# A hybrid decoder step with 32 experts: the last expert's block written out behind TensorE's loop, and the samples' final sums laid over 128 partitions behind the first prompt tile's

## The chip, the cores and the metric

The kernel runs on one NeuronCore of a Trainium2 chip. Its time is the device time of one execution in microseconds (us), the median of several runs. A page of the profile and a trace come from one execution recorded by the hardware profiler. Engines: TensorE (PE, with PEld for its weight loads), VectorE (DVE), ScalarE (ACT), GpSimd (POOL) and SyncE (SP); the suffix q means the engine's sequencer (SPq issues DMAs). L12 is line 12 of the kernel.

## What is computed

One layer over 512 prompt rows and 8 sample rows (one new token for each of 8 sequences), all in float32, 1024 wide. Attention and convolution come first; they are not touched here. The part at issue is the mixture of experts and its last sum:

```python
def _layer_tail(x, attn, conv, w_out, norm2_w, router_w, router_b, ...):
    x = x + jnp.concatenate([attn, conv], axis=-1) @ w_out
    h = _rmsnorm(x, norm2_w).reshape(B * S, D)
    return x + _moe(h, router_w, router_b, w_gate_up, b_gate_up, w_down, b_down).reshape(B, S, D)

def _moe(...):          # 32 experts, each row goes to the 4 best
    gates = softmax(the 4 largest router logits of a row)
    for each expert e:  # rows that chose e
        gu = xb @ w_gate_up[e] + b_gate_up[e]         # 1024 x 2048
        act = (clip(gu[:, F:]) + 1) * min(gu[:, :F], 7) * sigmoid(1.702 * g)
        y = act @ w_down[e] + b_down[e]               # 1024 x 1024
    return sum over a row's 4 experts of gate * y
```

An expert's weights are 8 MB (gate and up) and 4 MB (down), so the 32 experts read 400 MB.

## The kernel before, in words

**Experts.** Work is organised in blocks of at most 128 rows, one block per expert (E = 32), plus up to OVF = 16 late blocks for experts that more than 128 rows chose; with these inputs there are none, but each engine still steps through a loop of 16 passes (`Fori(0, OVF)` with an `If` inside: L2122 to L2127 on DVE) and skips each body. Block i's rows are gathered from `h2_rows` in DRAM by GpSimd (`gather`, L733), multiplied by gate and up weights (`gate_up_front` L1509 for rows 0 to 63, `gate_up_back` L1528 for rows 64 to 95 and 96 to 127, skipped by `by_size` where the block has no such rows), clipped and multiplied on DVE and ACT, transposed (L1616) and multiplied by the down weights (`down_front` L1546, `down_back` L1557). DVE (`copy_y`, L2079 and L2080) and ACT (`copy_y`, L1153, eight small copies) take the result from PSUM to `y_sb`, and GpSimd scatters its rows to `y_rows` in DRAM (`scatter`, L744).

**TensorE's order.** `expert_block(i, i - 1)` does gate and up of block i, transposes the rows of block i + 1, does down of block i - 1 and transposes the activations of block i. Blocks 0 and 1 are written out, `pe.Fori(2, E)` runs blocks 2 to 31, and `down_block(E - 1, ...)` behind the loop does the last down with weights in buffers of their own (`last_down_front`, `last_dn`). DVE, ACT, POOL and SP have loops of their own over the same blocks. A down of block i waits until both `copy_y` of block i - 1 are done (`y_front`, `y_back`).

**Weights.** SP loads them in chunks of 2 MB: four chunks of gate and up (L573), two of down (L578), each waiting for its buffer (`w_used`); the last down has its own two loads (L629). Behind these SP queues five loads of the residual rows `x2_rows` into `out_acc` (L633), waits for the last down (L638), steps through the loop of 16, waits for the last scatter, and issues five loads of `y_rows` into `out_rows` (L650).

**The last sum.** `out_rows[u]` has, for each row of tile u, its 4 expert rows side by side; `gates` has the 4 gates of each row. DVE makes, for each tile u and each of the 4 choices, one `scalar_tensor_tensor`: acc = rows * gate + acc (L2135). Tiles 0 to 3 are the four prompt tiles of 128 rows, tile 4 (`TILES`) the 8 sample rows. `OUT_ORDER = [TILES] + list(range(TILES))` sets the order of the loads (SP), sums (DVE) and stores (ACT, L1175): samples first, then prompt tiles 0 to 3.

Of the kernel before, what the change touches and what calls it, by code (L numbers as in the profile page):

```python
# [7 lines left out]
P = 128  # L8
D = 1024
# [45 lines left out]
def hybrid_step(nc, x_prompt, x_sample, cache_k, cache_v, state_conv, page_table, norm1_w, w_in,  # L55
# [10 lines left out]
    with ctx:  # L66
# [140 lines left out]
        out_acc = [v_flat[:, u * D:(u + 1) * D] for u in range(TILES)] + [q_b[:, :, :].rearrange("p a n -> p (a n)")]  # L207
# [141 lines left out]
        y_stored, x2_back, gu_done = [sem(n) for n in ("y_stored", "x2_back", "gu_done")]  # L349
# [133 lines left out]
        OUT_ORDER = [TILES] + list(range(TILES))  # L483
# [5 lines left out]
        def _(sp):  # L489
# [141 lines left out]
            sp.wait_ge(late_slots_done, 1)  # L631
            for u, s in enumerate(TAIL):
                sp.dma_start(out_acc[u][0:rows_of(s), :], x2_rows[row0[s]:row0[s] + rows_of(s), :]  # L633
                             ).then_inc(x2_back, 16)
# [13 lines left out]
            for u in OUT_ORDER:  # L648
                r, m = row0[TAIL[u]], rows_of(TAIL[u])
                sp.dma_start(out_rows[u][0:m, :],  # L650
                             y_rows[r * TOPK:(r + m) * TOPK, :].rearrange("(p k) n -> p (k n)", k=TOPK)
                             ).then_inc(y_loaded[u], 16)
# [123 lines left out]
        def _(act):  # L776
# [396 lines left out]
            for no, u in enumerate(OUT_ORDER):  # L1173
                act.wait_ge(pair_done, TOPK * (no + 1))
                act.dma_start(y_out[TAIL[u]], out_acc[u][0:rows_of(TAIL[u]), :]).then_inc(y_stored, 16)  # L1175
# [3 lines left out]
        def _(pe):  # L1179
# [421 lines left out]
            def expert_block(i, before=None, front=gate_up_front, back=gate_up_back):  # L1601
# [8 lines left out]
                if before is not None:  # L1610
                    down_block(before, isinstance(i, int))
# [25 lines left out]
            with pe.Fori(2, E) as i:  # L1637
                expert_block(i, i - 1)
            down_block(E - 1, False, last_down_front, last_down_back)
# [9 lines left out]
        def _(dve):  # L1649
# [480 lines left out]
            dve.wait_ge(x2_back, 16 * (TILES + 1))  # L2130
            for no, u in enumerate(OUT_ORDER):
                m, acc = rows_of(TAIL[u]), out_acc[u]
                dve.wait_ge(y_loaded[u], 16)
                for k in range(TOPK):
                    nc.vector.scalar_tensor_tensor(acc[0:m, :], out_rows[u][0:m, k * D:(k + 1) * D],  # L2135
                                                   gates[0:m, u, k:k + 1], acc[0:m, :], ALU.mult, ALU.add
                                                   ).then_inc(pair_done, 1)
                    dve.wait_ge(pair_done, no * TOPK + k + 1)
# [44 lines left out]
```

## Time and profile before

| what | value |
|---|---|
| time, median of 3 runs | 1743.2 us (1741.07 to 1750.26) |
| profiled execution, its own time | 1743.68 us |
| its span in the trace | 1742.0 us |
| PE busy | 1464.7 us (84%) |
| DVE busy | 781.1 us (45%) |
| ACT busy | 356.1 us (20%) |
| HBM read and written | 589.36 MB and 25.87 MB |

Times inside the trace run from the span's start to 1742.0. The experts take the stretch from about 665 us to 1700 us, the last sum the 42 us behind it. Busy time is an average over stages with different limits; the waits, the chain that ended last and the DMA landings tell what a stretch is limited by.

### The profile page before, as it was taken

The numbers are of one execution on the slowest core, as the hardware profiler recorded it, in microseconds if no ns is written. First come the engines' busy times: TensorE is split into PE (matmuls) and PEld (weight loads), VectorE is DVE, ScalarE is ACT, GpSimd is POOL, SyncE is SP. The second block draws the span as 40 slices with busy tenths as digits, with TensorE's granted clock in tenths as the row PEclk, the third lists the DMA queues.
The fourth block names the chain that finished last, engine by engine and source line by source line (L and its number), as shares of the span: only waits on it lengthen the run. The fifth ranks groups of instructions, "written<-read, shape, count | busy, mean of one in ns | idle before, by whom it ended". The sixth has DMA issues, their size and how long they took to land.

```text
span 1742.0 us, 32083 instructions
## 1 busy us (share of the span) xinstructions
PE 1464.7 (84%) x11950; PEld 589.3 (34%) x11951; DVE 781.1 (45%) x1158; ACT 356.1 (20%) x822; POOL 95.4 (5%) x173
## 2 busy tenths in 40 slices
PE   3868886768898868999999898999998998998870
PEld 2433332335433343333333332332333332332220
DVE  2789877997886335211323222232232131131316
ACT  3212202232320221111211211211212122121220
POOL 0000002000000000000000000000000000000000
PEclk8989996688998857999999999999999999999995
DMA  9558798878989765579999999999999999999976
GB/s 326 190 176 270 268 356 289 262 258 282 332 295 308 253 257 216 234 312 404 428 418 415 427 399 397 426 404 395 418 423 402 410 428 394 402 428 428 427 324 251
DMA packets 127181, 598.10 MB, mean 343 GB/s; under 512 B 20392, under 2 KB 20406, under 8 KB 101915
## 3 DMA queue, kind: packets, MB, share of 16 engines
q1 hardware_dynamic: 109088, 560.20, 81.5%
q10 hardware_dynamic: 8522, 20.00, 3.2%
q0 software_dynamic: 9504, 17.06, 2.6%
q8 instruction: 37, 0.61, 0.1%
q14 instruction: 30, 0.24, 0.0%
HBM read 589.36 MB, written 25.87 MB: 353 GB/s over the span
## 4 chain that ended last, share of the span: by engine, by line
PE 39%; DMA 20%; DVE 2%; issue 1%; ACT 0%; DVEq 0%; SPq 0%; ACTq 0%
PE bank L1509 23%; DMA wts<-in_w_gate_up 14%; PE bank L1546 8%; DMA wts<-in_w_down 6%; PE bank L1528 4%; DVE v_ring L2135 1%; PE bank L1499 1%; PE bank L1616 1%; PE bank L1557 1%; PE bank L1597 0%; DVE q_b L2135 0%; DMA h_tok<-h_rows,v_tok 0%; ACT k_T L1153 0%; DVEq L2123 0%; ACT k_T L1136 0%
## 5 line engine op out<-in xcount | busy, mean ns | idle before, releaser
L1509 PE MATMUL bank<-wts,h_T 128*32 128x512 f32 x4032 | 444.0, 596 | 17.9 <-DMA wts<-in_w_gate_up 17.9
L2057 DVE TENSOR_SCALAR q_T<-bank 128x512 f32<-128x512 f32 x32 | 22.1, 692 | 636.2 <-PE bank L1509 636.2
L1546 PE MATMUL bank<-wts,k_T 128*32 128x512 f32 x2048 | 229.7, 599 | 9.6 <-issue 4.9
L1509 PEld LDWEIGHTS bank<-wts,h_T 128*32 128x32 f32 x4032 | 129.3, 111 | 317.9 <-issue 288.3
L1656 DVE TENSOR_TENSOR wts<-wts,q_b 128x1024 f32<-128x1024 f32 x128 | 157.6, 1231 | 23.6 <-DMA wts<-in_cache_k 17.3
L1528 PE MATMUL bank<-wts,h_T 128*32 128x512 f32 x992 | 129.1, 662 | 45.6 <-DMA wts<-in_w_gate_up 43.8
L1659 DVE TENSOR_REDUCE sc<-wts 128x16 f32<-128x1024 f32 x128 | 156.2, 1220 | 4.4
L1143 ACT ACTIVATE h_T<-bank 128x512 f32<-128x512 f32 x66 | 35.9, 595 | 571.5 <-PE bank L1499 571.5
L1546 PEld LDWEIGHTS bank<-wts,k_T 128*32 128x32 f32 x2048 | 65.3, 111 | 151.7 <-issue 138.8
L1221 PE MATMUL bank<-wts,h_T 128*8 128x128 f32 (+1 forms) x480 | 91.9, 449 | 13.1 <-DMA wts<-in_w_in 7.1
L1153 ACT ACTIVATE k_T<-bank 32x256 f32<-32x256 f32 x256 | 95.8, 374 | 14.6 <-PE bank L1546 11.2
L1221 PE MATMUL bank<-wts,mix 128*128 128x512 f32 x160 | 73.9, 616 | 6.9 <-DVE u_tok L1656 6.9
L1370 PE MATMUL bank<-wts,mix 128*128 128x512 f32 (+1 forms) x256 | 68.3, 493 | 5.7 <-DVE mix L1656 4.1
L1136 ACT ACTIVATE k_T<-bank 128x512 f32<-128x512 f32 x64 | 34.9, 595 | 186.5 <-PE bank L1616 186.5
L1528 PEld LDWEIGHTS bank<-wts,h_T 128*32 128x32 f32 x992 | 30.1, 115 | 126.5 <-DMA wts<-in_w_gate_up 65.0
L1477 PE MATMUL bank<-v_ring,ex 128*8 128x512 f32 x320 | 50.6, 710 | 22.7 <-DMA v_ring<-in_cache_v 12.0
L1221 PEld LDWEIGHTS bank<-wts,h_T 128*8 128x8 f32 (+1 forms) x480 | 42.5, 144 | 60.6 <-issue 57.4
L1557 PE MATMUL bank<-wts,k_T 128*32 128x256 f32 x1024 | 58.8, 381 | 0.2 <-DMA wts<-in_w_down 0.2
L2079 DVE COPY k_T<-bank 64x512 f32<-64x512 f32 x32 | 21.9, 683 | 74.2 <-PE bank L1546 73.8
L731 POOL COPY v_tok<-v_tok 128x1 int32 (+1 forms) x34 | 6.2, 183 | 793.2 <-PE bank L1499 522.5
L1221 PEld LDWEIGHTS bank<-wts,mix 128*128 128x128 f32 x160 | 30.7, 197 | 46.9 <-issue 46.9
L2058 DVE TENSOR_SCALAR qk<-bank 64x512 f32<-64x512 f32 x64 | 44.4, 694 | 2.2
(328 smaller groups left out, 1361.1 us busy)
## 6 DMA issues: line engine op xcount, KB each, us to landing
wts<-in_w_gate_up SPq DMA_DIRECT2D x126, 2048.0 KB, 15.4
wts<-in_w_down SPq DMA_DIRECT2D x64, 2048.0 KB, 18.2
wts<-in_cache_k SPq DMA_DIRECT2D x256, 256.0 KB, 3.6
v_ring<-in_cache_v SPq DMA_DIRECT2D x160, 256.0 KB, 3.9
wts<-in_cache_v SPq DMA_DIRECT2D x96, 256.0 KB, 3.8
wts<-in_w_in SPq DMA_DIRECT2D x5, 2048.0 KB, 24.1
wts<-y_rows SPq DMA_DIRECT2D x4, 2048.0 KB, 15.0
wts<-in_w_out ACTq DMA_DIRECT2D x1, 4096.0 KB, 19.9
```

Of the source, the lines that this page charges most:

```text
L1143: nc.scalar.activation(hg_T[:, 4 * q:4 * q + 4, :], t_view(TB[q], P), ACT.Copy).then_inc(xt_copied, 1)
L1153: m = nc.scalar.activation(y_sb[64 + 32 * b:96 + 32 * b, 256 * q:256 * (q + 1)], PS[5][32 * q:32 * q + 32, 256 * b:256 * (b + 1)], ACT.Copy)
L1221: m = nc.tensor.matmul(out, h_T_of(("P", s))[:, kt, 0:n], w_in_sb[:, c, kt, c0:c0 + cols], start=(kt == 0), stop=(kt == KT - 1))
L1370: m = nc.tensor.matmul(out, mix_T[:, kt, r:r + n], w_out_sb[:, kt, c0:c0 + cols], start=(kt == 0), stop=(kt == KT - 1))
L1477: last = nc.tensor.matmul(U[32 * q:32 * q + HC, :], ex[:, n, :], v_of(m)[:, p, :], start=(n < 4), stop=(n >= PAGES - 4 and q > 0))
L1509: m = nc.tensor.matmul(PS[part][p0:p0 + 32, :], lhs[:, 32 * b:32 * b + 32], rhs[:, part * F + half * 512:part * F + half * 512 + 512], sta ...
L1528: nc.tensor.matmul(PS[2 + b][p0:p0 + 32, :], lhs[:, 64 + 32 * b:96 + 32 * b], rhs[:, part * F + half * 512:part * F + half * 512 + 512], s ...
L1546: m = nc.tensor.matmul(PS[4][p0:p0 + 32, :], act_T[0][:, k, a0:a0 + 32], chunk[c][:, k, n * 512:(n + 1) * 512], start=(c == 0 and k == 0), ...
L1557: nc.tensor.matmul(PS[5][32 * q:32 * q + 32, 256 * b:256 * (b + 1)], act_T[1][:, k, a0:a0 + 32], chunk[c][:, k, q * 256:(q + 1) * 256], st ...
L1656: return nc.vector.tensor_tensor(out, a, b, ALU.mult)
L1659: return nc.vector.tensor_reduce(out, src, X, ALU.add)
L2058: last = nc.vector.tensor_scalar(u_out, u, LIMIT, -LIMIT, ALU.min, ALU.max)
```

## The change

Four things change.

- TensorE's loop runs over blocks 2 to 30; `expert_block(E - 1, E - 2)` is written out behind it. The argument `first` of `down_block` now asks for `before == 0`, so that the written-out block still waits for `y_front` and `y_back`.
- The samples' last sum is laid out differently. Each of the 8 rows is cut in `SPLIT` = 16 pieces of 64 columns, so that (row, piece) fills 128 partitions, and one `scalar_tensor_tensor` works on 128x64 instead of 8x1024. The load of the samples' `y_rows` becomes 8 DMAs, one per sample, each of 16 partitions with 4 runs of 64 floats (256 bytes). The residual rows and the store are cut in the same way (`by_piece`).
- The gates of a sample must lie on its 16 partitions. SP writes them to DRAM (into rows of `slot_table`, no longer needed by then), waits for that write, and reads them back spread over 16 partitions each (`gates_split`). Both stand in SP's order ahead of the loads of the residual rows. Their landings are counted by `sums_in`, which takes the place of `x2_back`.
- `OUT_ORDER` becomes [0, 4, 1, 2, 3]: the first prompt tile's loads, sums and store come first, the samples' second.

```diff
@@ SP
             sp.wait_ge(x2_out, 16 * (TILES + 1))
             sp.wait_ge(late_slots_done, 1)
+            gate_rows = slot_table[0:NB * TOPK, :].rearrange("(b k) o -> b (k o)", k=TOPK)
+            sp.dma_start(gate_rows, gates[0:NB, TILES, :].bitcast(i32)).then_inc(sums_in, 16)
+            sp.wait_ge(sums_in, 16)
+            sp.dma_start(gates_split.bitcast(i32), gate_rows.unsqueeze(1).to_broadcast([NB, SPLIT, TOPK])
+                         ).then_inc(sums_in, 16)
             for u, s in enumerate(TAIL):
-                sp.dma_start(out_acc[u][0:rows_of(s), :], x2_rows[row0[s]:row0[s] + rows_of(s), :]
-                             ).then_inc(x2_back, 16)
+                rows = x2_rows[row0[s]:row0[s] + rows_of(s), :]
+                sp.dma_start(out_acc[u], rows if s else by_piece(rows)).then_inc(sums_in, 16)
...
             for u in OUT_ORDER:
                 r, m = row0[TAIL[u]], rows_of(TAIL[u])
-                sp.dma_start(out_rows[u][0:m, :],
-                             y_rows[r * TOPK:(r + m) * TOPK, :].rearrange("(p k) n -> p (k n)", k=TOPK)
-                             ).then_inc(y_loaded[u], 16)
+                rows = y_rows[r * TOPK:(r + m) * TOPK, :]
+                if u < TILES:
+                    sp.dma_start(out_rows[u], rows.rearrange("(p k) n -> p (k n)", k=TOPK)).then_inc(y_loaded[u], 16)
+                else:
+                    for b in range(NB):
+                        sp.dma_start(out_rows[u][b * SPLIT:(b + 1) * SPLIT, 0:TOPK * D // SPLIT].rearrange("c (k n) -> c k n", k=TOPK),
+                                     rows[b * TOPK:(b + 1) * TOPK, :].rearrange("k (c n) -> c k n", c=SPLIT)
+                                     ).then_inc(y_loaded[u], 16)
@@ ACT
-                act.dma_start(y_out[TAIL[u]], out_acc[u][0:rows_of(TAIL[u]), :]).then_inc(y_stored, 16)
+                act.dma_start(y_out[TAIL[u]] if u < TILES else by_piece(y_out[0]), out_acc[u]).then_inc(y_stored, 16)
@@ PE
-                    down_block(before, isinstance(i, int))
+                    down_block(before, isinstance(before, int) and before == 0)
...
-            with pe.Fori(2, E) as i:
+            with pe.Fori(2, E - 1) as i:
                 expert_block(i, i - 1)
+            expert_block(E - 1, E - 2)
             down_block(E - 1, False, last_down_front, last_down_back)
@@ DVE
-            dve.wait_ge(x2_back, 16 * (TILES + 1))
+            dve.wait_ge(sums_in, 16 * (TILES + 3))
             for no, u in enumerate(OUT_ORDER):
-                m, acc = rows_of(TAIL[u]), out_acc[u]
-                dve.wait_ge(y_loaded[u], 16)
+                acc, cols = (out_acc[u], D) if u < TILES else (out_acc[u], D // SPLIT)
+                gate = gates[:, u, :] if u < TILES else gates_split
+                dve.wait_ge(y_loaded[u], 16 if u < TILES else 16 * NB)
                 for k in range(TOPK):
-                    nc.vector.scalar_tensor_tensor(acc[0:m, :], out_rows[u][0:m, k * D:(k + 1) * D],
-                                                   gates[0:m, u, k:k + 1], acc[0:m, :], ALU.mult, ALU.add
-                                                   ).then_inc(pair_done, 1)
+                    nc.vector.scalar_tensor_tensor(acc, out_rows[u][:, k * cols:(k + 1) * cols], gate[:, k:k + 1], acc,
+                                                   ALU.mult, ALU.add).then_inc(pair_done, 1)
```

## Rows read from the trace of the kernel before

**Rows 1.** Chain that ended last: start us, us, what. Pieces from 1688 us on.
```profile
1688.28 0.39 ACT k_T L1153
1688.66 1.17 issue
1689.84 10.02 PE bank L1546 x64
...
1712.47 0.05 issue
```

**Rows 2.** Timeline of DVE, last two lines: start us, us, instruction, idle before.
```profile
1712.60 5.20 DVE L2135 SCALAR_TENSOR_TENSOR q_b<-wts,w_T,q_b 8x1024 f32<-8x1024 f32 x4 [11.31 <-DMA wts<-y_rows]
1717.83 21.10 DVE L2135 SCALAR_TENSOR_TENSOR v_ring<-wts,w_T,v_ring 128x1024 f32<-128x1024 f32 x16
```

**Rows 3.** DMA issues in narrow windows: prompt tiles 0 and 3, last number us to landing.
```profile
wts<-y_rows SPq DMA_DIRECT2D x1, 2048.0 KB, 8.2
...
wts<-y_rows SPq DMA_DIRECT2D x1, 2048.0 KB, 22.9
```

**Rows 4.** Timeline of SP in the same windows: issue of tiles 0 and 3.
```profile
1708.42 0.35 SPq L650 DMA_DIRECT2D wts<-y_rows  x1
...
1709.76 0.98 SPq L650 DMA_DIRECT2D wts<-y_rows  x1
```

**Rows 5.** Windows over the last loads: last columns PEclk, DMA share, GB/s.
```profile
1709.00:1710.00 1.00, 0.00 (x0) 0.00 (x0) 0.00 (x0) 0.00 (x0) 0.00 (x0) 0.50 1.56 279
...
1714.00:1722.00 8.00, 0.00 (x0) 0.00 (x0) 7.79 (x7) 0.00 (x0) 0.00 (x0) 0.50 1.01 430
```

**Rows 6.** Timeline of PE: downs of blocks 30 and 31; POOL before the scatter of 30.
```profile
1675.43 3.64 PE L1546 MATMUL bank<-wts,k_T 128*32 128x512 f32 x32
1680.11 3.64 PE L1546 MATMUL bank<-wts,k_T 128*32 128x512 f32 x32 [1.04 <-DMA wts<-in_w_down]
1689.84 9.98 PE L1546 MATMUL bank<-wts,k_T 128*32 128x512 f32 x64 [4.92 <-issue]
...
1689.61 0.18 POOL L742 COPY v_tok<-v_tok 128x1 int32 x1 [11.31 <-ACT k_T L1153]
```

**Rows 7.** Windows around the last down: last columns PEclk, DMA share, GB/s.
```profile
1690.00:1694.00 4.00, 4.00 (x20) 0.81 (x20) 0.00 (x0) 0.00 (x0) 1.01 (x1) 0.50 0.50 196
...
1696.00:1700.00 4.00, 3.81 (x36) 1.18 (x28) 0.12 (x1) 0.12 (x1) 0.00 (x0) 1.00 0.02 4
```

**Rows 8.** Timeline of SP: last down's loads, residual rows, the long wait.
```profile
1658.26 5.25 SPq L629 DMA_DIRECT2D wts<-in_w_down  x2
...
1665.45 3.67 SPq L633 DMA_DIRECT2D q_b<-x_rows  x1
1708.06 2.68 SPq L650 DMA_DIRECT2D wts<-y_rows  x5
```

**Rows 9.** DMA issues in narrow windows: last down's loads; the scatter before last.
```profile
wts<-in_w_down SPq DMA_DIRECT2D x1, 2048.0 KB, 26.7
...
y_rows<-k_T,v_tok POOLq DMA_INDIRECT x1, 5.7
```

**Rows 10.** Groups by form: VectorE operations nearest to 128x64.
```profile
L1774 DVE SCALAR_TENSOR_TENSOR rot<-qk,stq,rot 128x128 f32<-128x128 f32 x4 | 1.4, 351 | 0.1
...
L2018 DVE SCALAR_TENSOR_TENSOR k_T<-k_T 128x32 f32<-128x32 f32 x3 | 0.6, 192 | 0.1
```

**Rows 11.** DMA queues in 3 to 6, 6 to 10, 700 to 780 us: packets, MB, share of 16 engines.
```profile
q10 hardware_dynamic: 222, 0.05, 6.9%
...
q1 hardware_dynamic: 585, 1.20, 80.8%
...
q8 instruction: 7, 0.11, 0.6%
```

**Rows 12.** Timeline of PE in straight code: down of block 0, back half and front.
```profile
723.88 3.66 PE L1557 MATMUL bank<-wts,k_T 128*32 128x256 f32 x64
727.36 7.05 PE L1546 MATMUL bank<-wts,k_T 128*32 128x512 f32 x64
```

More of the change, by code:

```diff
@@ L206, in hybrid_step, with by_piece @@
         out_rows = [wts[:, u * TOPK * D:(u + 1) * TOPK * D] for u in range(TILES + 1)]
-        out_acc = [v_flat[:, u * D:(u + 1) * D] for u in range(TILES)] + [q_b[:, :, :].rearrange("p a n -> p (a n)")]
+        out_acc = [v_flat[:, u * D:(u + 1) * D] for u in range(TILES)] + [q_b[:, 0, 0:NB * D // P]]
+        SPLIT = P // NB
+        gates_split = v_tok[:, 1, 132:132 + TOPK]
+        def by_piece(rows):
+            return rows.rearrange("b (c n) -> (b c) n", c=SPLIT)
         TAIL = [1, 2, 3, 4, 0]
@@ L348, in hybrid_step @@
         bias_hi, bias_rest = [sem(n) for n in ("bias_hi", "bias_rest")]
-        y_stored, x2_back, gu_done = [sem(n) for n in ("y_stored", "x2_back", "gu_done")]
+        y_stored, sums_in, gu_done = [sem(n) for n in ("y_stored", "sums_in", "gu_done")]
         ids_done, entry_done, entry_summed, slot_part = [sem(n) for n in (
@@ L482, in hybrid_step @@
                                     mix[:, 0:SLOT].rearrange("p (k n) -> p k n", k=2)]
-        OUT_ORDER = [TILES] + list(range(TILES))
+        OUT_ORDER = [0, TILES] + list(range(1, TILES))
         last_dn = [w_slot[CHUNK_SLOT[c]].rearrange("p (k n) -> p k n", k=4) for c in range(2)]
```

## The prediction

> **What bounds the kernel now.** I read the chain of waits first, from its end. It shows that the edits can only touch two places. Up to 1680 us the chain is DMA: the down weights of block 30 arrive at 1680.1 and TensorE, which had waited 1.04 us, works at once [rows 6]. Then comes the last expert: TensorE stands for 4.92 us in front of the last down [rows 6], because `y_back` of block 30 comes only with ACT's eighth copy, at 1688.28 + 0.39 = 1688.67; 1.17 us later the first matmul starts [rows 1]. Behind the last down come the copies, the scatter, SP's loads of `y_rows` from 1708.06 [rows 8], and VectorE's 20 sums from 1712.60 to 1717.83 + 21.10 = 1738.93 [rows 2]. The last store and the end take 1742.0 - 1738.9 = 3.1 us.
>
> The question for the tail is what paces the sums, VectorE or the loads. The landings answer it. Tile 0 was issued at 1708.42 and took 8.2 us [rows 3, 4], so it landed at 1716.6; tile 3 was issued at 1709.76 and took 22.9, so 1732.7. VectorE's four sums of a tile take 21.10 / 4 = 5.28 us, so it began tile 0 at 1717.83 and tile 3 at 1738.93 - 5.28 = 1733.65 [rows 2]. VectorE is the one that is late, but by 1.2 us at tile 0 and 1.0 us at tile 3 only. The DMA engines are full behind them, at 430 GB/s from 1714 on [rows 5]; a tile of 2.1 MB needs 4.9 us there. So both run at nearly the same pace, and time taken from VectorE is worth at most the 1.0 us by which tile 3 waits for it, unless the loads come earlier as well. The samples' four sums cost 5.2 us [rows 2], but they run in a stretch in which no prompt tile is there yet: that is the point of this case.
>
> **The samples' sums.** Removed: four operations of 8x1024, 5.23 us from the first start to tile 0's start [rows 2]. Added: four of 128x64. Of the same operation, 128x128 takes 351 ns and 128x32 takes 192 [rows 10]; on the line between them 64 columns take 192 + 32 x 1.66 = 245 ns, and with the step of 1.32 - 1.285 = 0.035 us between dependent sums (21.10 / 16 = 1.32) four take 1.1 us. VectorE's own work falls by 4.1 us.
>
> **The order.** Samples first, VectorE could start at 1712.60, when its skipping loop was through (the chain shows its sequencer up to 1712.5 [rows 1]). Now its first work is tile 0, and that is not there. Tile 0 is issued first, at 1708.06 instead of 1708.42, and no longer has the samples' 0.13 MB ahead of it (0.3 us at 430 GB/s [rows 5]): 1716.6 - 0.36 - 0.3 = 1715.9. Bounds: 1716.6 if nothing is gained, since the rates in the first microseconds are uneven (279 GB/s at a share of 1.56 for 1709 to 1710 [rows 5]); 1714.5 if the slow start belonged to the samples' 8 rows. I take 1716.0.
>
> **The loads behind it.** Between tile 0 and tile 1 now stand 8 issues instead of none, with 8 x 16 x 4 = 512 pieces of 256 bytes. The trace has no such load. The nearest rows are of the first microseconds: 222 packets of about 225 bytes took 6.9% of 16 engines over 3 us, 3.3 us or 15 ns each; 585 packets of about 2 KB took 80.8% over 4 us, 52 us or 88 ns each [rows 11]. Over 16 engines, 32 pieces each, that is 0.5 to 2.8 us. The small row is the nearer one in size; pieces cut out of rows of 4 KB may cost more, so I take 30 ns, 1.0 us, and keep both ends. For the last tile the balance is then -0.36 - 0.3 + 1.0 = +0.3 us: tile 3 lands at 1733.0 instead of 1732.7.
>
> The Trainium skill, "DMA: Bandwidth & Descriptors" (Specifications), says that transfers below 512 bytes don't reach line rate because the engine reads, modifies and writes. It speaks against this change; at half the rate the 0.13 MB would cost an estimated 0.6 us instead of 0.3, less than the 1.0 taken above, and no run here shows the rule yet.
>
> **Sum of the tail.** By VectorE: 1716.0 + 0.1 + 5.28 (tile 0) + 1.1 (samples) + 3 x 5.28 = 1738.3. By the loads: 1733.0 + 0.1 + 5.28 = 1738.4. Both bounds agree, against 1738.93: the tail gains 0.5 us. Of the 4.1 us taken from VectorE, 3.5 go to its later start. Ends: -1.5 with cheap pieces and an early tile 0 (then tile 3's landing holds it), +1.5 with pieces of 88 ns and tile 0 at 1716.6. The stores change nothing: the last one is still tile 3's.
>
> **The gates' way through DRAM.** SP issues the write behind the last down's loads at about 1663.6 and waits. What is queued behind this wait: the read of the gates, five loads of residual rows, and, far off, the loads of `y_rows`. The write stands in SP's queue behind the last down's second chunk, issued about 1663.2 and landing 26.7 us later, at 1689.9 [rows 8, 9]. If it lands with that, at about 1690 to 1692, the read and the five loads are issued within 2.7 us (as five were at 1708 [rows 8]), and their 2.1 MB need 4.9 us: there by about 1699.5. SP is wanted at 1699.9, when the last down ends, VectorE asks for the rows at 1712.5. So the round trip is hidden, with 5 us to spare for SP's issues and 13 us for the data. One neighbour matters: the scatter of block 30, issued at 1690.59 and landing 5.7 us later [rows 9] at 1696.3; `copy_y` of block 31 waits for it at 1699.9. The residual rows now fall beside it instead of before it; its slack of 3.6 us covers the 1.2 us that 0.5 MB take at full rate, and again as much. Cost 0, bounds 0 to +2.
>
> **TensorE's written-out block.** The same instructions run in the same order with the same waits, 1 pass fewer in the loop. The loop's end moves from about 1684.9, in front of the 4.92 us wait, to about 1654, in a stretch that waits for weights: the second half of down 30 waited 1.04 us for its chunk [rows 6]. In the old place its cost, if any, lay under ACT's copies: the wait for `y_back` ends at 1688.67 whatever TensorE's sequencer did before. What could be visible is part of the 1.17 us behind it. That stretch also holds the load of the block's size into a register and two skipped branches, which stay. I take 0. The bound below: 1.17 us saved, and with it at most the 2.7 us that the last down loses to the clock, for it takes 9.98 us where two chunks at the full clock take 2 x 3.64 = 7.28 [rows 6]; the granted clock falls to 0.50 (1.2 GHz) before 1690 after 5 us of standing still and is back at 1.00 (2.4 GHz) in 1696 to 1700 [rows 7]. Bound above: +3 us, if fetching the longer straight code holds TensorE between 1674 and 1689, where only 1.04 us are free.
>
> **Sum.** -0.5 (tail) + 0 (gates) + 0 (TensorE) = -0.5 us against the profiled execution's 1743.68 us, so 1743.2. The median of the runs is 1743.2, 0.5 lower, which gives 1742.7. I forecast 1742.7 us.
>
> **Rivals.**
>
> *A, slower: SP's eight issues starve the queue.* Issues of `y_rows` took 0.35 to 0.98 us [rows 4]. Tile 1 follows tile 0 by nine of them: 1711.2 at 0.35, 1716.9 at 0.98. Tile 0's data are through at about 1715, the samples' at 1716, and packets begin about 1 us after an issue [rows 5, 8]. So it decides at 0.77 us per issue, when tile 1 is issued at 1715. At 0.98 the hole is 2 us, and with pieces of 88 ns another 2: tile 3 lands at 1735 to 1737, and the time is 1745 to 1747. For it: the one issue of 0.98, and the one of 3.67 us at 1665, behind loads that waited in the queue [rows 8]. Against: all five took 2.68 us together [rows 8], 0.43 each without that one.
>
> *B, slower: the straight code stalls TensorE.* Block 31 has no rows above 64, so its code jumps over both back halves twice. If each jump waits for code, 1 to 4 us are lost where 1 is free: 1744 to 1746. Against: blocks 0 and 1 are straight code as well. The down of block 0 jumps over its second back half, and its front starts at 727.36, with the end of the first back half (723.88 + 3.66 = 727.54, ends being modelled) [rows 12]: no gap, while 700 to 780 us fetched 7 packets of code [rows 11].
>
> The Trainium skill, "Runtime: NRT & Kernel Launch" (Instruction fetch mechanics), says that a taken branch whose target isn't held yet makes the sequencer fetch it before it goes on. By that rule, B happens if 31's jumps leave what is held, and the forecast holds if not.
>
> *C, faster: the last down starts sooner.* The 1.17 us shrink, and the clock's dip with them: 1742.7 - 1.17 = 1741.5, or 1738.8 with all of the dip. Against it: POOL, which has no loop's end there (it is at block 30, inside its own loop), starts at 1689.61, 0.94 us after the same eighth copy [rows 1, 6], so most of the 1.17 needs no loop's end; and the second chunk lands at 1689.9 anyway [rows 9].
>
> *D: the change is not felt at all* on the tail since tile 0 lands at 1716.6: 1743.3. It lies in the forecast's own range.
>
> **How the numbers follow.** Forecast (with D), 1741 to 1744: 0.65. A: 0.14. B: 0.08. C: 0.09. The rest, 0.04, is for both sides. The range also has to carry the runs' own scatter: the three of before lie between 1741.07 and 1750.26. I take 1738.8 to 1747.0: it takes in A and B nearly whole, and the nearer part of C. A difference of 0.5% is 8.7 us, about what a measurement of this kernel can tell from no change. No case reaches it by its own working; what is left is several of them together, or a scattered run: faster 0.03, same 0.93, slower 0.04.
>
> **What would show it.** Right: VectorE's first sum is tile 0's, at 1716.0 within 0.7; the samples' four take 1.1 us together; the last sum ends 0 to 1.5 us earlier measured from SP's first load of `y_rows`; TensorE stands 4.5 to 5.3 us before the last down, clock 0.50 behind it. Wrong: tile 1 issued later than 7 us after tile 0 (A); gaps of TensorE inside 1654 to 1689 that were not there, beginning at a jump (B); a standstill before the last down under 4 us (C); VectorE or SP waiting for `sums_in`, which would make the gates' way visible.

## The result, and the profile after

| what | value |
|---|---|
| the changed kernel, median of 18 runs | 1751.29 us (1745.02 to 1755.91) |
| the kernel before, median of 18 runs on the same chips | 1744.78 us (1740.56 to 1750.38) |
| ratio | 1.0035, 95% interval 1.0022 to 1.0047: 6.1 us slower (3.8 to 8.2) |
| profiled execution of the changed kernel | 1755.04 us, span 1753.3 us |

The 6.1 us follow from the ratio; the two medians alone lie 6.5 us apart. The forecast was 1742.7 us in a range of 1738.8 to 1747.0. The median lies 4.3 us above the range and 8.6 us above the forecast. Of these 8.6 us, 1.6 are the starting point: the forecast began from the 1743.2 us of three runs of before, and 18 runs of it give 1744.8. The rest is what the change did and the 0.5 us that it was to gain.

The two profiled executions can't be subtracted from the span's start: single runs of one kernel differ by 10 us, and by block 30 these two differ by 6 us already, in a stretch in which they do the same. So I measure all traces from one event just in front of the written-out block, TensorE's second transposes of block 30's activations. I call its start **the mark**. First the row of before, then that of after (timeline of PE):

```profile
1653.60 0.65 PE L1616 MATMUL bank<-ident,rot 128*128 128x128 f32 x4
```

```profile
1659.66 0.65 PE L1632 MATMUL bank<-ident,rot 128*128 128x128 f32 x4
1660.44 1.48 PE L1525 MATMUL bank<-wts,h_T 128*32 128x512 f32 x9
1664.10 6.21 PE L1525 MATMUL bank<-wts,h_T 128*32 128x512 f32 x55 [2.19 <-issue]
...
1680.60 1.16 PE L1515 MATMUL bank<-ident,h_tok 128*128 128x128 f32 x8
1684.72 7.07 PE L1562 MATMUL bank<-wts,k_T 128*32 128x512 f32 x64 [2.97 <-issue]
...
1697.87 9.69 PE L1562 MATMUL bank<-wts,k_T 128*32 128x512 f32 x64 [4.91 <-issue]
```

There are two holes that before doesn't have: TensorE stops after 9 matmuls of gate and up 31 for 2.19 us, and in front of down 30 for 2.97 us, each time for "issue", that is for nothing that the profile shows. In front of the last down the 4.91 us are the old ones. The last down starts 38.2 us behind the mark; before it was 1689.84 - 1653.60 = 36.2 [rows 6].

Behind the last down, the chain that ended last, then SP's and VectorE's timelines of after, which answer to [rows 8] and [rows 2]:

```profile
1712.46 5.47 DMA y_rows<-k_T,v_tok
```

```profile
1670.94 0.34 SPq L639 DMA_DIRECT2D slot_table<-w_T  x1
1696.35 0.69 SPq L641 DMA_DIRECT2D v_tok<-slot_table  x1
...
1717.94 0.33 SPq L663 DMA_DIRECT2D wts<-y_rows  x1
1718.33 5.10 SPq L666 DMA_DIRECT2D wts<-y_rows  x8
1723.47 1.38 SPq L663 DMA_DIRECT2D wts<-y_rows  x3
```

```profile
1727.12 5.25 DVE L2153 SCALAR_TENSOR_TENSOR v_ring<-wts,w_T,v_ring 128x1024 f32<-128x1024 f32 x4 [18.07 <-DMA wts<-y_rows]
1732.40 1.25 DVE L2153 SCALAR_TENSOR_TENSOR q_b<-wts,v_tok,q_b 128x64 f32<-128x64 f32 x4
1733.88 5.25 DVE L2153 SCALAR_TENSOR_TENSOR v_ring<-wts,w_T,v_ring 128x1024 f32<-128x1024 f32 x4 [0.23 <-DMA wts<-y_rows]
1739.44 5.25 DVE L2153 SCALAR_TENSOR_TENSOR v_ring<-wts,w_T,v_ring 128x1024 f32<-128x1024 f32 x4 [0.30 <-DMA wts<-y_rows]
1744.99 5.25 DVE L2153 SCALAR_TENSOR_TENSOR v_ring<-wts,w_T,v_ring 128x1024 f32<-128x1024 f32 x4 [0.30 <-DMA wts<-y_rows]
```

The last scatter takes 5.47 us to land, before it was 3.3 to 3.4 (SP's first load follows it, 1708.06 [rows 8]). SP's eight small issues take 5.10 us. VectorE begins with tile 0 9.2 us behind SP's first load and then waits a little for every prompt tile: now the loads pace it. The last sum ends at 1750.24, 32.3 us behind that load; before it was 1738.93 - 1708.06 = 30.9.

Step by step behind the mark, after against before: last down starts 38.2 against 36.2 (+2.0), its copies start at 48.0 against 46.3 (+1.7), SP's first load at 58.3 against 54.5 (+3.8, of which 2.1 are the scatter), last sum ends at 90.6 against 85.3 (+5.3), span ends at 93.6 against 88.4 (+5.2). That agrees with the 6.1 us (3.8 to 8.2) of the timed runs. So three things are to be explained: the holes, the slow scatter, and the loads.

### The profile page after: what moved, and what is told of

It is laid out like the page before. It is cut to its first block, busy times and chain, and to the rows that moved or that the text cites. A ratio compares the mean times of both kernels' runs of the same rounds, so it can differ in the third digit from the quotient of the medians.

```text
span 1753.3 us, 32079 instructions
## 1 busy us (share of the span) xinstructions
PE 1478.4 (84%) x11950; PEld 592.1 (34%) x11951; DVE 777.2 (44%) x1158; ACT 355.8 (20%) x822; POOL 95.3 (5%) x173
## 3 DMA queue, kind: packets, MB, share of 16 engines
q1 hardware_dynamic: 109992, 560.21, 81.1%
## 4 chain that ended last, share of the span: by engine, by line
PE 38%; DMA 22%; issue 1%; SPq 0%; ACT 0%; DVE 0%; POOLq 0%; ACTq 0%; POOL 0%; DVEq 0%
PE bank L1525 24%; DMA wts<-in_w_gate_up 20%; PE bank L1562 7%; PE bank L1544 4%; PE bank L1515 1%; DMA wts<-y_rows 1%; PE bank L1632 1%; PE bank L1573 1%; DMA y_rows<-k_T,v_tok 0%; PE bank L1613 0%; DVE v_ring L2153 0%; ACT k_T L1169 0%; SPq L666 0%; DMA h_tok<-h_rows,v_tok 0%; SPq L663 0%
## 5 line engine op out<-in xcount | busy, mean ns | idle before, releaser
L1525 PE MATMUL bank<-wts,h_T 128*32 128x512 f32 x4032 | 448.2, 600 | 16.3 <-DMA wts<-in_w_gate_up 14.0
L1544 PE MATMUL bank<-wts,h_T 128*32 128x512 f32 x992 | 131.1, 671 | 45.7 <-DMA wts<-in_w_gate_up 43.9
L1159 ACT ACTIVATE h_T<-bank 128x512 f32<-128x512 f32 x66 | 35.9, 595 | 576.3 <-PE bank L1515 576.3
L1237 PE MATMUL bank<-wts,h_T 128*8 128x128 f32 (+1 forms) x480 | 97.0, 478 | 11.5 <-ACT h_T L869 5.9
```

The source lines that it names most:

```text
L1159: nc.scalar.activation(hg_T[:, 4 * q:4 * q + 4, :], t_view(TB[q], P), ACT.Copy).then_inc(xt_copied, 1)
L1237: m = nc.tensor.matmul(out, h_T_of(("P", s))[:, kt, 0:n], w_in_sb[:, c, kt, c0:c0 + cols], start=(kt == 0), stop=(kt == KT - 1))
L1525: m = nc.tensor.matmul(PS[part][p0:p0 + 32, :], lhs[:, 32 * b:32 * b + 32], rhs[:, part * F + half * 512:part * F + half * 512 + 512], sta ...
L1544: nc.tensor.matmul(PS[2 + b][p0:p0 + 32, :], lhs[:, 64 + 32 * b:96 + 32 * b], rhs[:, part * F + half * 512:part * F + half * 512 + 512], s ...
```

## The experiments

Theory 1: TensorE waits for code in the written-out block. Theory 2: the loss is all in the new sums. The table holds what was measured. Its first columns come from one profiled execution of each kernel: the two holes of TensorE in the written-out block, then times in us behind the mark (start of the last down, start of its copies, SP's first load of `y_rows`, end of the last sum, end of the span). The last column comes from the timed runs: the ratio to before and its 95% interval, in us of 1745. Before was timed anew beside each group of experiments.

| kernel | holes of TensorE | last down | copies | first load | last sum | span | timed, us against before |
|---|---|---|---|---|---|---|---|
| before | none | 36.2 | 46.3 | 54.5 | 85.3 | 88.4 | |
| changed | 2.19, 2.97 | 38.2 | 48.0 | 58.3 | 90.6 | 93.6 | +6.1 (3.8 to 8.2) |
| e8_changed_again | 4.29, 3.08 | 38.9 | 48.8 | 58.7 | 91.1 | 94.3 | +4.7 (2.4 to 7.2) |
| e9_late_fetch | 2.52, 4.03 | 40.6 | 50.5 | 58.7 | 90.2 | 93.3 | +4.2 (1.4 to 7.2) |
| e1_pe_only | 2.93, 2.58 | 39.5 | 48.0 | 56.2 | 87.1 | 90.1 | +5.1 (2.8 to 7.3) |
| e10_pe_only_again | 2.43, 4.25 | 40.7 | 50.5 | 58.7 | 89.6 | 92.6 | +3.7 (1.2 to 6.3) |
| e7_half_skipped | none | 36.2 | 44.6 | 54.7 | 85.4 | 88.5 | +1.4 (-1.0 to 3.7) |
| e3_no_skipped_code | none | 35.9 | 45.8 | 54.0 | 84.8 | 87.9 | +0.2 (-2.1 to 2.4) |
| e11_changed_no_skipped_code | none | 36.2 | 44.8 | 53.0 | 84.6 | 87.7 | -0.5 (-3.1 to 2.1) |
| e2_sums_only | none | 36.1 | 45.8 | 54.0 | 85.3 | 88.4 | 0.0 (-2.3 to 2.1) |
| e4_samples_last | none | 36.1 | 45.3 | 53.5 | 85.9 | 87.8 | -1.9 (-3.7 to 0.0) |
| e5_own_banks | none | 33.2 | 42.1 | 50.4 | 81.1 | 84.1 | -4.4 (-6.8 to -1.7) |
| e6_own_banks_samples_last | none | 32.6 | 41.4 | 50.0 | 82.1 | 84.1 | -5.2 (-7.3 to -3.0) |

**e1_pe_only, and again as e10_pe_only_again**: TensorE's part of the change alone.

```diff
-            with pe.Fori(2, E) as i:
+            with pe.Fori(2, E - 1) as i:
                 expert_block(i, i - 1)
+            expert_block(E - 1, E - 2)
-                    down_block(before, isinstance(i, int))
+                    down_block(before, isinstance(before, int) and before == 0)
```

> The kernel before with TensorE's block 31 written out behind its loop, and nothing else. Measured in the trace from TensorE's last transposes of block 30 (mark) on: before, the last down starts 36.2 us behind the mark and the span ends 88.4 behind it; in the changed kernel 38.2 and 93.6. Theory 1 (the straight code makes TensorE wait for code): two holes that the page calls issue, about 2 us after some matmuls of gate and up 31 and about 3 us in front of down 30, as the changed kernel has (2.19 and 2.97 us); the last down starts 38 to 38.5 us behind the mark; the kernel is 1.5 to 2.5 us slower than before, and 2 more if the code that TensorE fetches behind the last down is also what makes the last scatter land 5.5 us after its issue instead of 3.3. Theory 2 (the holes were chance of that one execution, the loss is all in the sums): no such holes, 36.2 us, time as before within 1 us.

Timeline of PE of e1_pe_only:

```profile
1658.08 1.47 PE L1509 MATMUL bank<-wts,h_T 128*32 128x512 f32 x9
1662.48 11.13 PE L1509 MATMUL bank<-wts,h_T 128*32 128x512 f32 x87 [2.93 <-issue]
...
1681.84 8.77 PE L1546 MATMUL bank<-wts,k_T 128*32 128x512 f32 x64 [2.58 <-issue]
...
1696.76 8.48 PE L1546 MATMUL bank<-wts,k_T 128*32 128x512 f32 x64 [4.99 <-issue]
```

The holes stand at the same two places, the first again after 9 matmuls. This part alone gives most of the loss (5.1 us, 2.8 to 7.3). In its first trace the span ended only 1.7 us late, as the last down took 8.48 us where before it took 9.98, so I ran it again.

> e1_pe_only itself again. Its first trace was 1.7 us behind that of before, its timed runs 5.0 (2.8 to 7.2). If the trace was a lucky one (a last down of 8.5 us where the others took 9.2 to 10, no code packet beside the scatter), this trace ends 90 to 92.5 us behind the mark, with the same two holes; time 3 to 6 us over before.

It came as expected: holes of 2.43 and 4.25 us, the span's end 92.6 us behind the mark. The mean of the five traces with the whole skipped code (changed, e8, e9, e1, e10) is 39.6 us for the last down, 3.4 more than before.

Not all of that is standing still. In e1, e9 and e10 the down behind the second hole took 8.5 to 8.8 us, and 7.07 in the changed kernel and in e8. The timeline's row and the clock column (behind the last pair of brackets) of e10 show why: TensorE had stood still for 4.25 us, and the granted clock was 0.51 over the next 3 us, close to the lower level of 1.2 GHz; over the down of the changed kernel it was 1.00.

```profile
1684.46 8.53 PE L1546 MATMUL bank<-wts,k_T 128*32 128x512 f32 x64 [4.25 <-issue]
```

```profile
1684.46:1687.50 3.04, 3.04 (x16) 0.78 (x20) 2.02 (x4) 0.00 (x0) 0.00 (x0) 0.51 1.00 403
```

For e1 the account is 2.58 (second hole) - 1.04 (the wait for weights that before has inside down 30, now over by then) + 1.70 (slower matmuls) = 3.2 us, and the last down starts 3.3 us later. The first hole hardly counts: gate and up 31 waits for weights anyway, and its last eight matmuls start 20.2 to 20.7 us behind the mark in all five, against 20.2 before.

**e2_sums_only**: the change without the edit above. In the text that follows the two theories are named the other way round: its theory 1 puts a loss into the sums, its theory 2 is that TensorE's part is the whole loss.

> The change without TensorE's part: loop to block 31 as before, samples' sums over 128 partitions, gates through DRAM, order 0, 4, 1, 2, 3. Theory 1: the last down starts 36.2 us behind the mark (TensorE's last transposes of block 30) as before; SP's eight issues take 5.1 us, so tile 1 is issued 5.5 us behind tile 0 and tile 3's sums begin 27.0 us behind SP's first load of y_rows instead of 25.6; the kernel is 1.4 us slower than before, or 3.5 if the slow landing of the last scatter (5.5 us) belongs to the residual rows and the gates' round trip that now come late. Theory 2 (TensorE's part is the whole loss): as before within 1 us. My forecast for this part was -0.5 us.

```profile
1705.70 0.34 SPq L663 DMA_DIRECT2D wts<-y_rows  x1
1706.09 4.51 SPq L666 DMA_DIRECT2D wts<-y_rows  x8
1710.64 1.44 SPq L663 DMA_DIRECT2D wts<-y_rows  x3
...
1714.65 5.25 DVE L2152 SCALAR_TENSOR_TENSOR v_ring<-wts,w_T,v_ring 128x1024 f32<-128x1024 f32 x4 [15.73 <-DMA wts<-y_rows]
1719.93 1.25 DVE L2152 SCALAR_TENSOR_TENSOR q_b<-wts,v_tok,q_b 128x64 f32<-128x64 f32 x4
1721.22 15.81 DVE L2152 SCALAR_TENSOR_TENSOR v_ring<-wts,w_T,v_ring 128x1024 f32<-128x1024 f32 x12
```

(Timelines of SP and DVE.) The sums change nothing that the timed runs can tell. VectorE begins 8.95 us behind SP's first load and doesn't wait again: 8.95 + 4 x 5.28 + 1.29 = 31.4, the trace has 31.3, 0.5 more than before. The scatter landed in 3.3 us. So the loss isn't in the sums alone, as theory 2 at the head of this section had it. The 1.4 us that I gave this part lie inside the interval of the timed runs; the trace speaks for less, as tile 3's sums begin 26.1 us behind the first load, where I had expected 27.0 and before it was 25.6.

**e3_no_skipped_code, and e11_changed_no_skipped_code**: which code does TensorE wait for? In the written-out block the code for rows above 64 is left out, with its branches; blocks 30 and 31 have no such rows with these inputs, so the same matmuls run. e3 does it in e1, e11 in the changed kernel.

```diff
-                size = by_size(front, back, i)
+                if isinstance(i, int) and i == E - 1:
+                    size = front(i)
+                else:
+                    size = by_size(front, back, i)
...
-                by_size(front, back, i, size)
+                if isinstance(i, int) and i == E - 2:
+                    front(i)
+                else:
+                    by_size(front, back, i, size)
```

> As e1_pe_only, but in the written-out block the code for rows above 64 (both back halves of gate and up 31 and of down 30, with their branches) is left out; with these inputs the blocks 30 and 31 have no such rows, so the same matmuls run. Theory 1a (a jump over code that isn't there yet makes TensorE wait): no holes of 2 to 3 us, last down 36.2 us behind the mark, time as before. Theory 1b (straight code is fetched too slowly whether or not something is jumped over): the holes stay, 38 us. Theory 2: no difference from e1_pe_only.

```profile
1658.11 3.64 PE L1509 MATMUL bank<-wts,h_T 128*32 128x512 f32 x32
...
1678.78 3.64 PE L1546 MATMUL bank<-wts,k_T 128*32 128x512 f32 x32
1683.59 3.64 PE L1546 MATMUL bank<-wts,k_T 128*32 128x512 f32 x32 [1.17 <-DMA wts<-in_w_down]
```

(Timeline of PE of e3_no_skipped_code.) Both holes are gone, only waits for weights are left, and the time is that of before. The block is written out here as well, so it isn't straight code as such, nor the loop's end, but the code that is jumped over, or the branch over it, for both are gone here. e7 keeps the branch.

> The changed kernel, but in the written-out block the code for rows above 64 is left out (those blocks have no such rows here). If the skipped code is the whole loss, no holes, and the time is that of e2_sums_only: as before within 2 us. If the written-out block and the new sums also hurt each other in some other way, 2 to 4 us over before without any hole.

With all else of the change in place the loss is gone too: -0.5 us (-3.1 to 2.1).

**e7_half_skipped**: the size of the jump. In the written-out block only the code for rows 96 to 127 is left out.

```diff
                     back(i, 0)
-                    with pe.If(size > 96):
-                        back(i, 1)
+                    if halves == 2:
+                        with pe.If(size > 96):
+                            back(i, 1)
```

> As e1_pe_only, but in the written-out block only the code for rows 96 to 127 is left out, so each jump passes over half as many instructions as there (136 instead of 272 in front of gate and up 31, 128 instead of 256 in front of down 30). If TensorE waits because a jump takes it beyond the code that is there (theory 1a), the half jump costs less: either one of the two holes goes, or both shrink; the last down starts 36.2 to 37.5 us behind the mark, time 0 to 2.5 us over before. If any jump in straight code costs its fetch, whatever its length, both holes stay at 2 to 3 us, the last down starts at 38 to 39.5, time 3 to 5 us over before.

```profile
1657.01 3.64 PE L1509 MATMUL bank<-wts,h_T 128*32 128x512 f32 x32
...
1678.00 3.64 PE L1546 MATMUL bank<-wts,k_T 128*32 128x512 f32 x32
1682.70 3.64 PE L1546 MATMUL bank<-wts,k_T 128*32 128x512 f32 x32 [1.06 <-DMA wts<-in_w_down]
```

(Timeline of PE.) With a jump of half the length there is no hole at either place, so it is not a price of each jump. The timed runs agree less sharply (+1.4 us, -1.0 to 3.7), and this trace has a loss of its own: its last scatter was slow (5.2 us, see e8), which its short last down (8.41 us) hides in the span.

When the code is fetched shows what TensorE waits for. Queue q8 carries code in packets of some 16 KB; first its row in the page of before (37 packets), then its row for 1659.5 to 1660.0 us in e1_pe_only, in which the hole begins (1658.08 + 1.47 = 1659.55), and for 1661.5 to 1662.0 in the changed kernel (hole from 1661.92):

```profile
q8 instruction: 37, 0.61, 0.1%
```

```profile
q8 instruction: 1, 0.02, 13.8%
```

```profile
q8 instruction: 1, 0.02, 12.7%
```

The packets' start times in the traces say more. At each of the ten holes in the five traces one q8 packet starts, and TensorE goes on 2.4 to 2.6 us behind that start: 2.4 and 2.5 in the changed kernel, 2.5 and 2.5 in e8, 2.5 and 2.6 in e9, 2.5 and 2.6 in e1, 2.4 and 2.6 in e10. What makes a hole long is a packet that starts late: in e8 it starts 1.8 us behind the beginning of the first hole (4.29 us in all), in e10 1.7 us behind that of the second (4.25 us); the traces don't show what held it. In e3_no_skipped_code packets start at 1661.8 and 1682.3 as well, and TensorE doesn't stop: there they come ahead of need. From 780 to 1690 us of before, through the whole loop, no code packet moves at all.

The Trainium skill, "Runtime: NRT & Kernel Launch" (Instruction fetch mechanics), says that code is fetched in blocks of 256 instructions, one ahead while the current one runs, and that a taken branch beyond what is held waits for its block. Two back halves are 272 instructions in front of gate and up 31 (136 matmuls, each with its weight load) and 256 in front of down 30, one half is 136 and 128. The two holes agree with that: jumps over 272 and 256 instructions have one, jumps over 136 and 128 have none, and no run has a length between.

But length alone doesn't decide. In front of the last down TensorE jumps over 256 instructions too, in every kernel here and in before, and there is no hole: the first matmul starts 1.2 to 1.3 us behind ACT's last copy in all eleven traces in which it waits for that copy, as in [rows 1]. Where the two holes stand fits another reading, that TensorE runs out of the code that is there before the next packet is through. The first hole stands behind 9 matmuls, the second directly behind the jump. Counting matmuls and weight loads only, the first hole begins 272 + 2 x 9 = 290 instructions behind the start of the skipped code. In e6, whose loop ends one block later, TensorE stops behind 17 matmuls of the last down, 256 + 2 x 17 = 290 instructions behind the start of the code skipped there, and goes on 2.2 us behind the start of a q8 packet (timeline of PE of e6_own_banks_samples_last):

```profile
1687.42 2.33 PE L1562 MATMUL bank<-wts,k_T 128*32 128x512 f32 x17 [1.75 <-issue]
1690.78 5.35 PE L1562 MATMUL bank<-wts,k_T 128*32 128x512 f32 x47 [1.03 <-issue]
```

In before these first matmuls ran at a granted clock of 0.50, 20 in 4 us [rows 7], and the packet that started at 1690.66 was in time. By this reading a long jump costs because it leaves little code to work on while the next packet comes. It is argued from these counts; no run moved the code's place with the jumps left as they are.

**e4_samples_last**: order 0, 1, 2, 3, 4 in e2.

```diff
-        OUT_ORDER = [0, TILES] + list(range(1, TILES))
+        OUT_ORDER = list(range(TILES)) + [TILES]
```

> As e2_sums_only, with loads, sums and stores in the order 0, 1, 2, 3, 4: the eight small issues stand behind tile 3's. Theory A (eight issues and their pieces between tile 0 and tile 1 delay the prompt tiles): tile 3 lands about 24.3 us behind SP's first load instead of 27.0, its sums end at 29.7, the samples' four sums (1.25 us) follow, last sum ends at 31.1 us against 32.3 in the changed kernel and 30.9 before. Rival (the loss is tile 0's slow landing, 9.1 us, wherever the pieces stand): tile 3 lands at 26.5 to 27, last sum ends at 33.3.

```profile
1710.78 2.46 SPq L663 DMA_DIRECT2D wts<-y_rows  x4
1713.28 3.93 SPq L666 DMA_DIRECT2D wts<-y_rows  x8
...
1719.27 15.81 DVE L2152 SCALAR_TENSOR_TENSOR v_ring<-wts,w_T,v_ring 128x1024 f32<-128x1024 f32 x12 [15.26 <-DMA wts<-y_rows]
1736.60 5.25 DVE L2152 SCALAR_TENSOR_TENSOR v_ring<-wts,w_T,v_ring 128x1024 f32<-128x1024 f32 x4 [1.52 <-DMA wts<-y_rows]
```

(Timelines of SP and DVE.) VectorE starts 8.49 us behind the first load instead of 8.95, but tile 3's sums begin 25.8 us behind it, where I expected its landing at 24.3 from one theory and at 26.5 to 27 from the other: neither was right. The last sum ends 32.35 us behind the first load. What is gained lies behind it, as the last store is now the samples' 32 KB: 1745.1 - 1743.1 = 2.0 us from the last sum to the span's end instead of 3.1. The timed gain of 1.9 us (0.0 to 3.7) touches zero.

**e8_changed_again, and e9_late_fetch**: the slow scatter. e8 is the changed kernel again. In e9 TensorE waits behind the last down before it goes through its 16 skipped bodies:

```diff
             down_block(E - 1, False, last_down_front, last_down_back)
+            pe.wait_ge(y_scattered, E * 16)
             pe.wait_ge(meta_out, 3)
```

> The changed kernel itself again, for a second trace. If the last scatter's 5.5 us to land belong to the change (code fetched and residual rows loaded near it), it lands in over 5 us again and the last sum ends 90 us or more behind the mark. If they were chance (e1_pe_only and e2_sums_only both had 3.2 to 3.3), it lands in 3.2 to 3.5 us, the holes of TensorE are there again, the last down starts 38 to 39.5 us behind the mark and the last sum ends at about 88. The time should again be 4 to 8 us over before.

The scatter was slow again: issued at 1710.23, SP's first load at 1715.39. So the 5.5 us were not chance. Of all traces three had a slow scatter (changed 5.5, e8 5.2, e7 5.2), and these three alone had a q8 packet that started 1 to 2 us behind its issue. In e5 and e6 one started 0.3 us behind it, and the scatter landed in 3.2 and 3.3 us as without one. The queue rows of the changed kernel for 1714 to 1715 us (code), and for 1716.46 to 1717.46 (the scatter's queue):

```profile
q8 instruction: 1, 0.02, 10.3%
```

```profile
q0 software_dynamic: 6, 0.02, 5.8%
```

Six packets of the scatter are still under way more than 4 us behind its issue; in before all 144 are through in 3 us.

> The changed kernel with one wait added: TensorE, done with the last down, waits for the last scatter to have landed before it steps through its 16 skipped bodies, so that the code it fetches for them cannot fall beside the scatter. In the three traces in which the last scatter took 5.2 to 5.5 us to land (the changed kernel twice, e7_half_skipped), a packet of code was fetched 1 to 2 us behind its issue; in the traces of before, e1, e2, e3 and e4, with 3.2 to 3.3 us, none was. Theory S (the code packet holds up one DMA engine's share of the scatter): the scatter lands in 3.2 to 3.4 us, SP's first load of y_rows comes 2 us sooner behind the last down; if the packets now fall beside tile 0's load, part of this is lost again there. The holes in front of the last down stay; time 2.5 to 4.5 us over before instead of 5 to 6. Rival (the slow scatter belongs to something else in the changed kernel, such as the holes or the clock): 5.2 us again and the same time as the changed kernel.

Issue and SP's first load in e9 (timelines of POOL and SP):

```profile
1712.04 0.99 POOL L760 DMA_INDIRECT y_rows<-k_T,v_tok  x1 [0.80 <-POOL v_tok L758]
```

```profile
1715.40 0.33 SPq L663 DMA_DIRECT2D wts<-y_rows  x1
```

No packet of the queue q8 starts between 1705 and 1720 us, and the scatter lands in 3.3 us. As the added wait is TensorE's, the packet that fell there was TensorE's code. The sums then end 31.5 us behind the first load, as in e2 (31.3) and e11 (31.6), not 32.3. So the effect on the scatter is shown, in one trace; on the time it isn't, since TensorE lost more in this execution than in the other two of the changed kernel (last down at 40.6 against 38.2 and 38.9) and the timed runs of e9 and of the changed kernel overlap.

The slow scatter doesn't follow from the holes: e1 and e10 have the holes and a scatter of 3.3 us, e7 has no hole and one of 5.2. Nor can the timed runs tell the changed kernel (+6.1 and +4.7) from TensorE's part alone (+5.1 and +3.7).

**e5_own_banks, and e6_own_banks_samples_last**: is the 4.9 us standstill before the last down on the path? The last down writes banks 0 and 1, free by then, and its copies go to `x_in`, so that it doesn't wait for block 30's copies (of the two `copy_y` only ACT's stands here, DVE's is changed alike).

```diff
-                down_front(0, last_dn, last_full)
+                down_front(0, last_dn, last_full, bank=PS[0])
-                down_back(0, b, last_dn, last_full)
+                down_back(0, b, last_dn, last_full, bank=PS[1])
...
-            down_block(E - 1, False, last_down_front, last_down_back)
+            down_block(E - 1, True, last_down_front, last_down_back)
+            pe.wait_ge(y_front, E)
+            pe.wait_ge(y_back, E)
...
-            copy_y(E - 1, False)
+            copy_y(E - 1, True, x_in, PS[1])
-            scatter(E - 1, False)
+            scatter(E - 1, False, x_in)
```

> The kernel before (loop to block 31, old sums), but the last down writes banks 0 and 1 instead of 4 and 5, and its copies go to a buffer of their own (x_in), so that it waits neither for the copies of block 30 nor, at its own copies, for the scatter of block 30. It tests the reading that the 4.9 us in front of the last down are a wait for ACT's eight copies and lie on the path. If so: the last down starts about 33 us behind the mark (TensorE's last transposes of block 30) instead of 36.2, its second chunk of weights (landing at 36.3) holds it for 0 to 1 us, the clock stays high or falls for a shorter time, its end comes at 40 to 41 instead of 46.3, and the kernel is 4.5 to 6 us faster. Rival: the 4.9 us are a wait for weights or for code behind the loop's end; then the last down starts at 35.5 or later and the gain is under 1.5 us.

```profile
1690.39 8.77 PE L1546 MATMUL bank<-wts,k_T 128*32 128x512 f32 x64 [1.71 <-issue]
```

(Timeline of PE.) The standstill falls from 4.92 to 1.71 us, the last down starts 3.0 us sooner, its copies 4.2 us, and the timed gain is 4.4 us (1.7 to 6.8), a little under the 4.5 to 6 expected. The reading of the chain was right.

> e4_samples_last (loop to block 31, new sums, order 0, 1, 2, 3, 4) with the last down of e5_own_banks. If both gains are real and lie behind one another, it is faster than before by the sum of e5_own_banks and e4_samples_last (2 us): 6 to 8 us. If the gates' round trip through DRAM, hidden so far behind the last down, comes to light once the last down ends 5 us earlier, SP issues the residual rows at about 40 us behind the mark and reaches the loads of y_rows late: then no more than e5_own_banks alone.

5.2 us faster than before (3.0 to 7.3), the fastest median of this study. The 6 to 8 us that I expected and the sum of both gains (6.3) are not reached, though the interval doesn't exclude 6.3; in its trace the 1.03 us shown above, by that reading a wait for code, stand inside the last down. The gates' round trip didn't come to light.

## Why the prediction was wrong, point by point

**TensorE's written-out block: the step that failed.** I took 0 for it and gave the stall (rival B) 0.08. In the evidence against B, the row was right and what I drew from it wrong. The down of block 0 jumps over one back half, 128 instructions, with no gap [rows 12]. The written-out block goes over both halves, 272 instructions in gate and up 31 and 256 in down 30. In its place the runs showed two waits for code of 2.2 to 4.3 us. e7 has neither with half of the code left out, and e3 and e11, with all of it left out, have nothing of the loss. B said itself that block 31 jumps over both; I didn't ask whether the row had a jump of that length. A row of that length would not have settled it either: the last down of before jumps over 256 instructions without a hole. B's price of 1 to 4 us was near for the last down's start (2.0 to 4.5 later in five traces, 3.4 in the mean), but less the 1 us that is free it gives 1742.7 to 1745.7 and not the 1744 to 1746 stated. The first hole is hidden by waits for weights. Of the second, in front of down 30, the 1.04 us that I called free are free, and in three of five traces the lower clock behind it adds 1.5 to 1.7 us, which no step had.

**Code as traffic, which no step had.** In the changed kernel a code packet falls beside the last scatter, which lands 1.8 to 2.1 us later in both of its traces; e9 keeps the packet away and has the 3.3 us back. I treated code fetching as TensorE's matter alone; it is traffic on the DMA engines. What this is worth in the timed runs stays open.

**The samples' sums.** Expected -0.5 us, measured 0.0 (-2.3 to 2.1) alone, and +0.5 in the stretch from the first load to the last sum. VectorE's four sums were expected at 1.1 us and took 1.25. The term that was mis-sized is tile 0's landing: I let it come 7.9 us behind SP's first load; VectorE began at 8.95 in e2, 9.2 in the changed kernel. Without pieces behind it (e4, e6) it began at 8.5, the very 8.54 that tile 0 had behind the samples' load (1716.6 - 1708.06 [rows 3, 8]). So being first gained nothing, the bound I kept, and with the pieces behind it tile 0 comes another 0.5 to 0.8 us later (8.95 to 9.25 in e2, the changed kernel, e8, e9 and e11), which I had put on tile 3 alone. All of VectorE's saved 4.0 us go to its later start, not most of it: in e2 it begins 4.4 us later behind the first load than before, which leaves the loss of 0.5. No run parts the pieces from their eight issues.

**Rival A** (eight issues starve the queue) put its point of decision at 0.77 us per issue. They took 0.56 in e2 and 0.64 in the changed kernel, the first of them 1.15 and 1.54, and tile 1 was issued 5.5 us behind tile 0 in the changed kernel, short of the 7 us named as A's sign. In e2 VectorE doesn't wait for tiles 1 to 3. In the changed kernel and in e8 it does, 0.2 to 0.4 us each, and the stretch is 32.3 and 32.4 us, each time with a q8 packet within 0.4 us of the first load; e9, with no q8 packet in the first 4 us behind its first load, has 31.5. That these packets make the difference is argued, not shown.

**The gates' way through DRAM** was hidden, as said: SP waited 25.1 us for the write, which landed at 1696.35, 36.7 behind the mark, and was done with the residual rows at 1700.03, before it was wanted at 1707.6. The scatter of block 30 landed after 7.7 us instead of 5.7, still 1.3 us before the copies that wait for it.

**Rival C** didn't happen; the standstill stayed at 4.9 to 5.0 us in every kernel that kept block 30's copies in front of the last down. That it is a wait for these copies was confirmed by e5.

**The range** had +3 us for TensorE, and the last down starts 2.0 to 4.5 us late. Beyond that it had nothing for the clock, the scatter or the slower loads, and it began 1.6 us too low. 1744.8 + 3 = 1747.8 would still be under the median of 1751.3.

## What to carry to other kernels

Writing out the last pass of a loop brings straight code, whose packets move while it runs. Count the instructions that each skipped branch in it passes over: by the reading above, which is argued, they shorten the time in which the next packet can come. A free jump elsewhere in the trace proves little, neither a shorter one (128 instructions here) nor one of the same length at another place (256 in front of the last down). What settles it is a trace with the branches left out of the written-out block, and the code packets beside TensorE's holes. Here the skipped code cost nothing inside the loop and about 4 to 6 us behind it. An operation that waits for its first tile gains nothing from having less work in front of it; ask first what the engine does at the moment at which the saved time falls.

## What the runs showed of the hardware that I had not expected

- TensorE's loop, with the same jumps in its body, ran from 780 to 1690 us without one code packet. The same body written out once had two holes of 2.2 to 4.3 us, and TensorE went on 2.4 to 2.6 us behind the start of a code packet at all ten of them in five traces.
- With a code packet of some 16 KB that started 1 to 2 us behind the issue of a scatter of 0.26 MB, the scatter landed in 5.2 to 5.5 us (three traces); with none there, or one 0.3 us behind the issue, in 3.2 to 3.4 (ten traces).
- The last down, 64 matmuls after 4.9 us of standing still, took 8.4 to 10.0 us in different executions, as the granted clock came back sooner or later: 8.41 us at a mean granted clock of 0.84 in e7, 9.98 at 0.71 in before. A single trace can be 1.5 us off from this alone.
